# Two decoder blocks on one core: memory queries and second-block latents projected from unscaled chunks, and large tiles placed on multiples of 128 bytes

## The chip, the cores and the metric

One core of one Trainium2 chip runs the whole program. The metric is the device time of one execution in microseconds, lower is better. TensorE does the matrix products, VectorE (DVE) and ScalarE (ACT) the elementwise work, GpSimd (POOL) splits the weights, and SyncE (SP) issues the weight loads.

## What is computed

Two transformer blocks over 512 tokens of width 1024, all in float32. What matters here, cut down:

```python
h = x + token_mixers(rms_norm(x, norm_mix), ...)
n, mem_n = rms_norm(h, norm_mem), rms_norm(mem, norm_mem_kv)       # 512 and 256 tokens
h = h + memory_cross_attention(n, mem_n, w_mem_q, w_mem_kv, w_mem_o)
h = h + conv_ffn(rms_norm(h, norm_ffn), w_up, conv_w, conv_b, w_down)
x1 = rms_norm(h, final_norm)                                       # end of the first block
n2 = rmsnorm(x1, norm_g_2)                                         # start of the second
q_lat, c_kv, k_rope, z_a, ..., q_idx, k_idx, w_idx, ... = split(n2 @ w_in_2)
q  = rmsnorm(q_lat, g_q_lat_2) @ w_uq_2
kv = rmsnorm(c_kv, g_kv_lat_2) @ w_ukv_2
```

A norm multiplies each token by one number (its token scale, one over the root of the mean square) and each feature by a gain. The token scale commutes with the product by a weight matrix, so `norm(h) @ W` may be had as `((h * gain) @ W) * scale`.

## The kernel before

**Layout.** Activations lie feature-major: a tile holds 128 features on the partitions and 512 tokens along the row. A width of 1024 is 8 such chunks (`DC`), the width 2816 of the feed-forward part is 22 (`FC`).

**The products.** Every float32 operand of a projection is split into a high part (float32r) and the remainder, and `three` (L528 to L530) issues high x high, low x high and high x low for each pair of chunks, 128x128 weights against 512 tokens (256 in the memory's key and value projections). `project` (L536 on) makes one output chunk of 128 features from 8 input chunks, so 24 matmuls; `down` takes 22 input chunks, so 66 matmuls. Output chunks alternate between two PSUM banks. `open_bank` lets TensorE start chunk g only when chunk g-2 has been read by the engine that consumes it (`out_of_bank`).

**The weights.** They come as one stream of slots of 512 KB in exactly the order in which TensorE uses them, the table `STREAM`. SP loads into a ring of four, POOL makes `wH` (L483) and `wL` (L485) in two buffers each, preceded by a small `tick` (L482). POOL may split slot n+2 only when TensorE is through with slot n. All three orders (SP, POOL, TensorE) are the same table.

**The activations' split.** DVE writes a value to `nt` (two buffers), ACT copies it to the high tile (`high`, L1110), and DVE subtracts to make the low tile (`low`, L1524). TensorE waits for the low part of input chunk k before it uses it in a stage's first output chunk.

**A norm.** ACT squares the chunks (`squares`, L1078), DVE adds them up (`accumulate`, L1533), TensorE sums over the partitions with a matrix of ones (`norm_sum`, L513), ACT takes the root (`deviation`, L1085), DVE the reciprocal (`inverse`, L1542), and then DVE multiplies (`normed`, L1546, the helper `norm`).

**The order around the first part of the change.** `mix_out` (8 output chunks, inputs `mgH`, `mgL`) ends the token mixer. Beside it DVE first norms the memory tokens in eight chunks (with the residual of output chunk 0 ahead of memory chunk 4, L1896), then adds the residuals of chunks 1 to 7 (L1586 from L1897). TensorE goes on with stages `mem0` to `mem3`, one per head: two key chunks, two value chunks, a query chunk (j = 4), a transpose of values (j = 5), a query chunk (j = 6), a transpose (j = 7). The queries of head 0 need the normed hidden chunks `nH`, `nL`, which DVE makes after the sum over all eight residual chunks (L1898, L1899). ACT copies the query chunks out of PSUM to `mq` (L1348), in its queue ahead of the values' copy. Heads 1 to 3 are projected beside the attention of the head before (`mem_beside`). The feed-forward's norm is already done in the other way: `with_gain` (L1904) makes the chunks with the gain alone beside `mem_o`, and DVE applies the token scale to the products (L1923, L1930).

**The order around the second part.** `down` ends the first block. After each of its eight chunks DVE adds the residual (L1952), ACT squares it, DVE multiplies the chunk by the final gain in place (L1955), ACT squares it again, and DVE adds both squares to two sums (L1946). After the last chunk TensorE sums both over the partitions (L513, L956), DVE forms the variance for the two norms together (L1963, L1964), ACT takes the root (L1397), DVE the reciprocal (L1966), and then DVE and ACT make the eight split chunks `mix2` (L1969, L1110, L1524) for the first projection of the second block, `q_idx`. The order on TensorE is: two small products for the bias table (L962, L963), `q_idx` (2 output chunks), `w_idx`, `k_idx`, a transpose, `q_lat` (3), `c_kv` (2), `k_rope`, `z_a`. ACT copies the latents to `qlat` and `ckv`. DVE also rewrites `hT` as the first block's output (L1976).

**Where tiles lie.** `place` gives each SBUF tile the next address that is a multiple of 32 bytes. `hT`, `nH`, `nL`, the ring, `wH` and `wL` come first and lie at multiples of 128. Behind them comes `vec` of 680 bytes, so all others lie 64, 96 or 32 bytes past such a multiple: `mgH`, `moH`, `aH`, `recH`, `attH` and their low parts at 64, `yaH`, `ybH`, `mg2H`, `qlH`, `ckH` and theirs at 32.

Of the kernel before, what the change touches and what calls it, by code (L numbers as in the profile page):

```python
# [20 lines left out]
ALU = mybir.AluOpType  # L21
# [62 lines left out]
    ("q_idx", [1] * 2), ("w_idx", [1]), ("k_idx", [1]), ("w_turn", [0]), ("q_lat", [1] * 3), ("c_kv", [1] * 2),  # L84
# [145 lines left out]
def build(nc, stream, xT, memT, pos, vecs, ident_d, const_r, const_a, const_d, sink_d, relb_d, gvec, x1_d, outT):  # L230
    with ExitStack() as ctx:
# [25 lines left out]
        sq0 = -(-top[0] // 32) * 32  # L257
        sq = place("sq", [P, 2, S])
        sums0 = -(-top[0] // 32) * 32
# [3 lines left out]
        nt = place("nt", [P, 2, S])  # L263
        sgb = place("sgb", [P, 2, S])
# [6 lines left out]
        OVER = top[0]  # L271
# [61 lines left out]
        aL = place("aL", [P, FC, S], F32R)  # L333
        gpad = place("gpad", [P, 2, S + 2])
        cv = place("cv", [P, 2, S])
        fu = place("fu", [P, 2, S])
        sums2 = place("sums2", [P, S], at=229344 - 4 * S)
# [9 lines left out]
        rl0 = -(-top[0] // 32) * 32  # L347
        rl = place("rl", [P, 2, S])
        late0 = top[0]
# [52 lines left out]

        def c_a(name, a, b):
            return cA[:, AT_A[name] + a:AT_A[name] + b]
# [21 lines left out]
        hg_made, var_made = sem("hg_made"), sem("var_made")  # L426
# [20 lines left out]
        gv_done, gv_out = sem("gv_done"), sem("gv_out")  # L447

# [47 lines left out]
        def _(pe):  # L496
# [41 lines left out]
            def project(stage, c0, n, xs, width=S, inputs=None):  # L538


                for c in range(c0, c0 + n):
                    out = open_bank(FIRST[stage] + c)[:, :width]
                    for k, x in enumerate(xs):
                        if k % BLK == 0:
                            r = open_slot()
                        if inputs is not None and c == c0:
                            pe.wait_ge(nl_made, SPLIT[inputs] + k + 1)
# [420 lines left out]
            project("q_lat", 0, 3, n_parts)  # L968
            project("c_kv", 0, 2, n_parts)
# [75 lines left out]
        def _(act):  # L1045
# [288 lines left out]
            highs("memory", mnH, DC, MEM)  # L1334
            squares("mem", hT, residual("mix_out"))

            def mem_out(h, j):
# [8 lines left out]
                else:  # L1346
                    c = 2 * h + (j - 4) // 2
                    copy_out(stage, j, mq[:, c, :])  # L1348
# [3 lines left out]
            mem_out(0, 1)  # L1352
            for c in range(DC):
                high("mem", c, nH[:, c, :])
                if c in (2, 5):
                    mem_out(0, 2 + c // 3)
            for j in range(4, 8):
                mem_out(0, j)

            def mem_beside(x):  # L1360
                h = x // ST + 1
                if h < MEM_HEADS:
                    for j in ((0, 1), (2, 3), (4, 5), (6, 7))[x % ST]:
                        mem_out(h, j)
# [889 lines left out]
```

## Time and profile before

| what | value |
|---|---|
| median of 3 runs | 1625.26 us (1623.28 to 1625.79) |
| the profiled execution | 1619.58 us |
| its span, first to last instruction | 1617.8 us |
| TensorE busy | 1505.2 us, 93% of the span |
| VectorE busy | 1042.5 us, 64% |
| GpSimd busy | 856.2 us, 53% |
| ScalarE busy | 472.4 us, 29% |
| granted TensorE clock, mean | 0.982 of full speed |

The profile is of one execution. Its time is 1.8 us more than its span, and it lies 5.7 us under the median of the runs. Busy shares are averages over stages with different limits. A matmul's duration in the trace overlaps its successor's, so the time that one takes away from TensorE is the distance from one start to the next, and a TensorE that is called busy all the time may still issue faster or slower.

### The profile page before, as it was taken

What the parts mean: (1) busy time and instruction counts of PE and PEld (TensorE: products, weight loads), DVE (VectorE), ACT (ScalarE), POOL (GpSimd) and SP (SyncE); (2) the same over time, 40 slices, a digit from 0 to 9 for tenths busy, and PEclk for the clock granted to TensorE, in tenths of its full rate; (3) what the DMA queues carried; (4) which work ended last, traced back from release to release, by engine and by line L of the source; (5) the groups of instructions that cost most, each with busy time, mean ns of one, the idle gap of its engine ahead of it and who ended that gap; (6) DMA issues with size and microseconds to landing.
All of it is one profiled execution on the core that took longest, in us unless ns stands there. A gap on an engine that the chain in (4) does not pass through costs nothing.

```text
span 1617.8 us, 20168 instructions
## 1 busy us (share of the span) xinstructions
PE 1505.2 (93%) x6988; PEld 1170.7 (72%) x6988; DVE 1042.5 (64%) x1907; ACT 472.4 (29%) x908; POOL 856.2 (53%) x690
## 2 busy tenths in 40 slices
PE   5989999899999899999999999988989999999996
PEld 3878777566777688678888887865847677666874
DVE  7477797887256632489999982337187788576234
ACT  3455432356212222321011010012252334354111
POOL 3523322433665677266767677673637443433664
PEclk9999999999999999999999999998999999999998
DMA  5211111211332333133333333332413531322331
GB/s 203 79 52 40 40 40 40 65 53 53 105 91 86 90 109 106 53 92 91 92 95 101 93 102 98 103 103 92 129 52 91 104 92 53 117 66 73 123 91 65
DMA packets 38315, 138.48 MB, mean 86 GB/s; under 512 B 4312, under 2 KB 4568, under 8 KB 37592
## 3 DMA queue, kind: packets, MB, share of 16 engines
q1 hardware_dynamic: 33408, 121.65, 24.9%
q10 hardware_dynamic: 4824, 15.69, 3.6%
q8 instruction: 56, 0.92, 0.3%
q14 instruction: 27, 0.22, 0.0%
HBM read 130.51 MB, written 6.82 MB: 85 GB/s over the span
## 4 chain that ended last, share of the span: by engine, by line
PE 77%; DVE 14%; issue 3%; ACT 3%; POOL 1%; PEld 0%; PEldq 0%; DMA 0%; ACTq 0%; DVEq 0%; POOLq 0%
PE pair L528 21%; PE pair L530 20%; PE pair L529 20%; PE pair L768 3%; PE pair L796 3%; PE pair L780 2%; DVE nt L1546 2%; PE pair L622 2%; PE pair L623 1%; DVE rstd L1542 1%; DVE nL L1524 1%; PE pair L984 1%; DVE kk L1737 1%; PE pair L670 1%; POOL wL L485 1%
## 5 line engine op out<-in xcount | busy, mean ns | idle before, releaser
L485 POOL TENSOR_TENSOR wL<-ring,wH 128x1024 fp32r<-128x1024 f32 x228 | 565.9, 2482 | 19.0
L528 PE MATMUL pair<-nH,wH 128*128 128x512 f32 x1120 | 452.4, 404 | 33.3 <-DVE nL L1524 15.4
L530 PE MATMUL pair<-nH,wL 128*128 128x512 f32 x1120 | 440.0, 393 | 0.0
L529 PE MATMUL pair<-nL,wH 128*128 128x512 f32 x1120 | 440.0, 393 | 0.0
L482 POOL TENSOR_TENSOR tick<-tick 128x1 f32<-128x1 f32 x228 | 55.9, 245 | 725.2 <-PE pair L530 716.0
L528 PEld LDWEIGHTS pair<-nH,wH 128*128 128x128 f32 x1120 | 211.8, 189 | 107.9 <-issue 30.0
L530 PEld LDWEIGHTS pair<-nH,wL 128*128 128x128 f32 x1120 | 212.3, 190 | 45.6
L483 POOL TENSOR_SCALAR wH<-ring 128x1024 fp32r<-128x1024 f32 x228 | 243.2, 1067 | 0.0
L529 PEld LDWEIGHTS pair<-nL,wH 128*128 128x128 f32 x1120 | 212.7, 190 | 41.5 <-issue 1.0
L1376 ACT ACTIVATE sgb<-cv 128x512 f32<-128x512 f32 x22 | 14.0, 634 | 208.8 <-DVE cv L1927 208.8
L528 PE MATMUL pair<-aH,wH 128*128 128x512 f32 x176 | 69.7, 396 | 0.0
L530 PE MATMUL pair<-aH,wL 128*128 128x512 f32 x176 | 69.6, 395 | 0.0
L529 PE MATMUL pair<-aL,wH 128*128 128x512 f32 x176 | 69.5, 395 | 0.0
L1658 DVE TENSOR_TENSOR X<-E,qT 128x64 f32<-128x64 f32 x224 | 40.4, 220 | 39.8 <-ACT E L1158 39.6
L1524 DVE TENSOR_TENSOR aL<-nt,aH 128x512 fp32r<-128x512 f32 x22 | 61.1, 2780 | 0.0
L1952 DVE TENSOR_TENSOR hT<-pair,hT 128x512 f32<-128x512 f32 x8 | 5.5, 692 | 81.0 <-PE pair L530 81.0
L1533 DVE TENSOR_TENSOR sums<-sums,sq 128x512 f32<-128x512 f32 (+1 forms) x38 | 36.5, 961 | 32.3 <-ACT sq L1078 30.9
L1926 DVE SCALAR_TENSOR_TENSOR cv<-gpad,vec,cv 128x512 f32<-128x512 f32 x22 | 56.7, 2578 | 0.8
L1586 DVE TENSOR_TENSOR hT<-pair,hT 128x512 f32<-128x512 f32 x24 | 16.5, 690 | 58.7 <-PE pair L530 58.7
L1158 ACT ACTIVATE E<-pair 128x896 f32<-128x896 f32 (+1 forms) x40 | 35.4, 937 | 61.4 <-PE pair L623 61.4
L1231 ACT ACTIVATE dx<-dx,stat 128x128 f32<-128x128 f32 (+3 forms) x64 | 36.0, 563 | 59.2 <-DVE stat L1785 59.0
L622 PE MATMUL pair<-cR,lftH 128*128 128x128 f32 (+1 forms) x144 | 43.4, 329 | 10.0 <-ACT Sg L1168 5.8
(339 smaller groups left out, 2738.9 us busy)
## 6 DMA issues: line engine op xcount, KB each, us to landing
ring<-stream SPq DMA_DIRECT2D x228, 512.0 KB, 3.6
gvec<-gv ACTq DMA_DIRECT2D x1, 2560.0 KB
hT<-xT SPq DMA_DIRECT2D x4, 512.0 KB, 5.4
x_d<-hT ACTq DMA_DIRECT2D x1, 2048.0 KB, 7.8
toep<-gvec ACTq DMA_DIRECT2D x8, 256.0 KB, 3.4
hT<-x_d ACTq DMA_DIRECT2D x1, 2048.0 KB, 8.6
outT<-hT ACTq DMA_DIRECT2D x8, 256.0 KB, 2.2
landing<-const_r ACTq DMA_DIRECT2D x1, 1216.0 KB, 6.3
```

The costliest lines, as they stand in the source:

```text
L482: pool.tensor_tensor(tick[:, 1:2], tick[:, 0:1], tick[:, 0:1], ALU.add).then_inc(high_done, 1)
L483: pool.tensor_scalar(wH[:, r % SPL, :], ring[:, r, :], 1.0, 0.0, ALU.mult, ALU.add).then_inc(high_done, 1)
L485: pool.tensor_tensor(wL[:, r % SPL, :], ring[:, r, :], wH[:, r % SPL, :].bitcast(F32), ALU.subtract).then_inc(split_done, 1)
L528: mm(out, a[0], b[0], start=first, stop=False)
L529: mm(out, a[0], b[1], start=False, stop=False)
L530: return mm(out, a[1], b[0], start=False, stop=last)
L622: mm(out, lftH[:, d, i, :], m, start=first, stop=False)
L768: last = mm(out, *pairs[t], start=t == 0, stop=t == count - 1)
L796: last = mm(out[rows, qs], w, turned[:, j % 2, t, qs], start=n_t == 0, stop=n_t == len(kind["serves"]) - 1)
L1524: V.tensor_tensor(lo[:, c, :], nt[:, k % 2, :width], hi[:, c, :].bitcast(F32), ALU.subtract).then_inc(nl_made, 1)
L1658: last = V.tensor_tensor(two(X[:, m % 2, kind, xs])[:, half], E[:, n % 2, b, ls].rearrange("p (b c) -> p b c", c=c), two(src)[:, half], AL ...
L1926: own(V.scalar_tensor_tensor(out=y, in0=x[:, 0:S], scalar=w[0], in1=y, op0=ALU.mult, op1=ALU.add))
```

## The change

1. **Memory queries.** The chunks for the memory queries are made with the gain alone (`with_gain`, now for both norms), beside `mix_out`: chunks 0 and 1 after the memory's norm, the others each after its residual. ACT makes the high parts there. DVE takes the query products out of PSUM, multiplied by the token scale (`mem_query`), for head 0 after `inverse("mem")` and for the others beside the attention's steps 2 and 3. ACT's query copies are gone.
2. **Residuals.** The residuals of chunks 0 and 1 of `mix_out` come ahead of the memory's norm chunks 4 and 6. Before, only that of chunk 0 came there.
3. **Second block.** After each `down` chunk ACT writes `uH`, the chunk times both gains (`g12`), and DVE its low part `uL`. `q_lat` and `c_kv` are projected from these, in the order: `q_lat` 0, the sums over the partitions, `q_lat` 1 and 2, `c_kv` 0 and 1, then the bias table, `q_idx` and on as before. The two sums meet in one PSUM bank through a third product with a matrix that holds EPS, so that L1963 and L1964 go, and ACT takes the root from the bank. DVE takes the latents out of PSUM times the token scale: `q_lat` 0 before the chunks of `mix2`, `q_lat` 1 and 2 after chunks 1 and 4, `c_kv` after the last one. `hT` is multiplied by both gain and scale at the end in place of L1955 and L1976.
4. **Placement.** Tiles of 512 bytes and more start at multiples of 128 bytes.

```diff
-    ("q_idx", [1] * 2), ("w_idx", [1]), ("k_idx", [1]), ("w_turn", [0]), ("q_lat", [1] * 3), ("c_kv", [1] * 2),
+    ("q_lat", [1] * 3), ("c_kv", [1] * 2), ("q_idx", [1] * 2), ("w_idx", [1]), ("k_idx", [1]), ("w_turn", [0]),
...
+        def aligned(size=512):
+            step = 128 if size >= 512 else 32
+            return -(-top[0] // step) * step
...
-            off = -(-top[0] // 32) * 32 if at is None else at
+            off = aligned(size) if at is None else at
...
+            u_parts = [(uH[:, k, :], u_low(k)) for k in range(DC)]
+            project("q_lat", 0, 1, u_parts, inputs="unscaled")
             pe.wait_ge(sq_added, ADDED["mix2"] + CHUNKS["mix2"] - 1)
+            pe.wait_ge(eps_set, 1)
             norm_sum("final")
-            mm(bank(6), ones[:, :], sums2[:, :], start=True, stop=True).then_inc(sum_done, 1)
+            mm(bank(6), ones[:, :], sums2[:, :], start=True, stop=False)
+            mm(bank(6), eps[:, :], sums[:, :], start=False, stop=True).then_inc(sum_done, 1)
+            project("q_lat", 1, 2, u_parts)
+            project("c_kv", 0, 2, u_parts)
...
-            highs("memory", mnH, DC, MEM)
-            squares("mem", hT, residual("mix_out"))
+            for c in range(DC):
+                high("memory", c, mnH[:, c, :], MEM)
+                if c in (3, 5):
+                    squares("mem", hT, residual("mix_out"), chunks=[c // 2 - 1])
+            for c in range(DC):
+                if c >= 2:
+                    squares("mem", hT, residual("mix_out"), chunks=[c])
+                high("mem", c, nH[:, c, :])
...
+                A(uH[:, c, :], hT[:, c, :], ACT.Copy, scale=g12[:, c:c + 1]).then_inc(uh_made, 1)
...
-            norm("memory", memx, "norm_mem_kv", mnH, mnL, MEM, lambda c: residual("mix_out", "mem", [0]) if c == 4 else None)
-            residual("mix_out", "mem", range(1, DC))
+            norm("memory", memx, "norm_mem_kv", mnH, mnL, MEM,
+                 lambda c: residual("mix_out", "mem", [c // 2 - 2]) if c in (4, 6) else None)
+            scale_queries = with_gain("mix_out", "mem", "norm_mem")
+            for c in range(2):
+                scale_queries(c)
+            residual("mix_out", "mem", range(2, DC), scale_queries)
+            low("mem", DC - 1, nH, nL)
...
+            def mem_query(h, b):
+                bk, free = product(f"mem{h}", 4 + 2 * b)
+                V.tensor_tensor(mq[:, 2 * h + b, :], bk, rstd[:, :], ALU.mult).then_inc(free, 1)
...
-            norm("mem", hT, "norm_mem", nH, nL)
+            def mem_beside(x):
+                if x % ST >= 2 and x // ST + 1 < MEM_HEADS:
+                    mem_query(x // ST + 1, x % ST - 2)
...
-                V.tensor_scalar(hT[:, c, :], hT[:, c, :], vcol("final_norm", c), None, ALU.mult).then_inc(hg_made, 1)
+                V.scalar_tensor_tensor(out=u_low(c), in0=hT[:, c, :], scalar=g12[:, c:c + 1], in1=uH[:, c, :].bitcast(F32),
+                                       op0=ALU.mult, op1=ALU.subtract).then_inc(ul_made, 1)
...
+            scaled("q_lat", 0, qlat)
             for c in range(DC):
-                V.scalar_tensor_tensor(out=open_split("mix2", c), in0=hT[:, c, :], scalar=vcol("norm_g_2", c),
-                                       in1=sums[:, :], op0=ALU.mult, op1=ALU.mult).then_inc(nt_made, 1)
+                V.scalar_tensor_tensor(out=open_split("mix2", c), in0=hT[:, c, :], scalar=g12[:, c:c + 1],
+                                       in1=sums2[:, :], op0=ALU.mult, op1=ALU.mult).then_inc(nt_made, 1)
                 if c:
                     low("mix2", c - 1, nH, nL)
+                if c in (1, 4):
+                    scaled("q_lat", 1 + c // 4, qlat)
             low("mix2", DC - 1, nH, nL)
+            for c in range(2):
+                scaled("c_kv", c, ckv)
```

## Rows read from the trace of the kernel before

**Rows 1.** The page: the engines of the chain that ended last, shares of the span

```profile
PE 77%; DVE 14%; issue 3%; ACT 3%; POOL 1%; PEld 0%; PEldq 0%; DMA 0%; ACTq 0%; DVEq 0%; POOLq 0%
```

**Rows 2.** The view by stretches: busy time (instructions) of each engine, granted clock, DMA

```profile
core 0: us, PE busy (x) PEld busy (x) DVE busy (x) ACT busy (x) POOL busy (x), PEclk, DMA share, GB/s
...
530.00:570.00 40.00, 31.24 (x169) 24.34 (x168) 25.02 (x24) 10.94 (x21) 26.75 (x21) 0.91 0.31 92
...
735.00:962.00 227.00, 226.54 (x999) 187.23 (x998) 210.60 (x168) 23.77 (x41) 161.84 (x125) 1.00 0.32 95
...
1086.00:1115.00 29.00, 16.10 (x43) 8.64 (x43) 23.01 (x24) 8.21 (x14) 5.28 (x6) 0.71 0.23 78
```

**Rows 3.** The view by tile, TensorE: count, duration min/median/max ns, first and last start

```profile
L529 PE MATMUL pair<-nL,wH x328: 387/389/396, 739.8 to 962.2; 128*128 128x512 f32 x164
...
L529 PE MATMUL pair<-aL,wH x176: 393/394/400, 962.9 to 1085.5; 128*128 128x512 f32 x176
...
L529 PE MATMUL pair<-moL,wH x64: 394/394/396, 675.1 to 719.2; 128*128 128x512 f32 x64
...
L529 PE MATMUL pair<-mg2L,wH x64: 392/397/400, 1556.8 to 1601.8; 128*128 128x512 f32 x64
```

**Rows 4.** Waits of TensorE, 486 to 568 us: us in total, times, longest

```profile
PE pair L528 <- ACT vraw L1066: 4.3, 1, 4.3
PE pair L528 <- DVE hT L1586: 2.4, 2, 1.2
```

**Rows 5.** Timeline of head 0's first query chunk, its weights' split, and the first scores

```profile
543.37 2.69 POOL L485 TENSOR_TENSOR wL<-ring,wH 128x1024 fp32r<-128x1024 f32 x1
...
545.05 0.28 PE L530 MATMUL pair<-mnH,wL 128*128 128x256 f32 x1
549.64 0.79 PE L528 MATMUL pair<-nH,wH 128*128 128x512 f32 x1 [4.30 <-ACT vraw L1066]
...
555.27 0.60 PE L530 MATMUL pair<-nH,wL 128*128 128x512 f32 x1
...
567.66 1.10 PE L768 MATMUL pair<-mk,mq 128*128 128x256 f32 x4 [0.83 <-ACT mv L1066]
```

**Rows 6.** The view by line: scores of the memory attention, all heads

```profile
L768 PE MATMUL pair<-mk,mq 128*128 128x256 f32 x64 | 16.7, 384 | 2.7 <-ACT mv L1066 2.7
```

**Rows 7.** Timeline of VectorE at the end of `mem_o`, where chunks are made unscaled

```profile
719.84 0.69 DVE L1586 TENSOR_TENSOR hT<-pair,hT 128x512 f32<-128x512 f32 x1 [0.61 <-PE pair L530]
...
724.16 1.48 DVE L1533 TENSOR_TENSOR sums<-sums,sq 128x512 f32<-128x512 f32 x2
```

**Rows 8.** Timeline from the end of `down` to the end of `k_rope`

```profile
1086.20 0.69 DVE L1952 TENSOR_TENSOR hT<-pair,hT 128x512 f32<-128x512 f32 x1 [10.02 <-PE pair L530]
...
1087.59 2.34 POOL L485 TENSOR_TENSOR wL<-ring,wH 128x1024 fp32r<-128x1024 f32 x1
1087.75 2.46 DVE L1955 TENSOR_SCALAR hT<-hT,vec 128x512 f32<-128x512 f32 x1 [0.86 <-ACT sq L1393]
...
1091.66 2.08 PE L513 MATMUL pair<-sums,ones 128*128 128x512 f32 x2 [5.50 <-DVE sums L1946]
...
1095.33 0.69 DVE L1963 TENSOR_SCALAR sums<-pair 128x512 f32<-128x512 f32 x1 [3.72 <-PE pair L956]
...
1097.44 3.35 DVE L1966 RECIPROCAL sums<-std 128x512 f32<-128x512 f32 x1 [0.69 <-ACT std L1397]
...
1103.11 0.77 PE L528 MATMUL pair<-nH,wH 128*128 128x512 f32 x1 [5.02 <-DVE nL L1524]
...
1112.00 3.34 DVE L1542 RECIPROCAL rstd<-std 128x512 f32<-128x512 f32 x1
...
1163.10 0.60 ACT L1066 ACTIVATE kp<-pair 128x512 f32<-128x512 f32 x1 [4.84 <-PE pair L530]
```

**Rows 9.** Bounds: float32 products at full clock, and VectorE's low parts beside a busy GpSimd

```profile
631.58 3.60 PE L796 MATMUL pair<-mPT,mv 128*128 128x512 f32 x8
...
L1524 DVE TENSOR_TENSOR aL<-nt,aH 128x512 fp32r<-128x512 f32 x22 | 61.1, 2780 | 0.0
```

More of the change, by code:

```diff
@@ L270, in build @@
         warm = place("warm", [P, len(NORMS)])
-        OVER = top[0]
+        g12 = place("g12", [P, DC])
+        OVER = top[0] = aligned()
         cA = place("cA", [P, COLS_A])
@@ L1413, in _ @@
             act.wait_ge(gv_out, 2)
-            for c in range(3):
-                copy_out("q_lat", c, qlat[:, c, :])
             squares("q_lat", qlat, lambda c: out_of_bank(act, FIRST["q_lat"] + c))
-            for c in range(2):
-                copy_out("c_kv", c, ckv[:, c, :])
             copy_out("k_rope", 0, kp[:, :])
@@ L1913, in _, with with_gain, use @@
-            residual("mem_o", "ffn", after=with_gain)
+            def with_gain(stage, name, gain):
+                def use(c):
+                    out = open_split(name, c)
+                    out_of_bank(dve, FIRST[stage] + c)
+                    V.tensor_scalar(out, hT[:, c, :], vcol(gain, c), None, ALU.mult).then_inc(nt_made, 1)
+                    if c:
+                        low(name, c - 1, nH, nL)
+                return use
+            norm("memory", memx, "norm_mem_kv", mnH, mnL, MEM,
+                 lambda c: residual("mix_out", "mem", [c // 2 - 2]) if c in (4, 6) else None)
@@ L1914, in _ @@
+            for b in range(2):
+                mem_query(0, b)
+            def mem_beside(x):
+                if x % ST >= 2 and x // ST + 1 < MEM_HEADS:
+                    mem_query(x // ST + 1, x % ST - 2)
+            attention("memory", mx, MEM_SCALE, lambda i: nomask[:, :], moH, moL, beside=mem_beside)
+            residual("mem_o", "ffn", after=with_gain("mem_o", "ffn", "norm_ffn"))
             low("ffn", DC - 1, nH, nL)
+            V.tensor_tensor(g12[:, :], vec[:, VEC["final_norm"]:VEC["final_norm"] + DC],
+                            vec[:, VEC["norm_g_2"]:VEC["norm_g_2"] + DC], ALU.mult).then_inc(gains_made, 1)
@@ L1956, in _, with scaled @@
             add_squares(DC - 1)
-            dve.wait_ge(sum_done, NORMS.index("mix2") + 1)
-            own(V.tensor_scalar(sums[:, :], bank(7), EPS, None, ALU.mult))
-            V.tensor_tensor(sums2[:, :], bank(6), sums[:, :], ALU.add).then_inc(var_made, 1)
             dve.wait_ge(std_made, NORMS.index("final") + 1)
-            V.reciprocal(sums[:, :], std[:, :]).then_inc(r_made, 1)
+            V.reciprocal(sums2[:, :], std[:, :]).then_inc(r_made, 1)
             dve.wait_ge(r_made, NORMS.index("final") + 1)
+            def scaled(stage, c, dst):
+                b, free = product(stage, c)
+                V.tensor_tensor(dst[:, c, :], b, sums2[:, :], ALU.mult).then_inc(free, 1)
```

67 lines of the change are left out of this document (30 added, 37 removed).

## The prediction

> **What bounds the kernel now.** I read the chain that ended last first, since a busy share says nothing of what would shorten the run. TensorE holds 77% of it and DVE 14% [rows 1]: most of the time the matmuls set the pace, and in a few places DVE does. The view by stretches shows where. In `up` TensorE is busy for 226.54 of 227 us, although DVE works 210.60 us beside it; from 1086 to 1115 us it is busy for 16.10 of 29 us at a granted clock of 0.71, and from 530 to 570 us for 31.24 of 40 at 0.91 [rows 2]. These two low places are the ones that the change rearranges. Third, the tile view, for the price of a matmul that nobody delays. A count with first and last start gives the distance: in `up`, which reads `nL` and `nH`, (962.2 - 739.8) / 327 triples = 0.680 us, or 226.7 ns a matmul; in `down`, which reads `aL` and `aH`, (1085.5 - 962.9) / 175 = 0.7006, or 233.5 ns; in `mem_o` (719.2 - 675.1) / 63, or 233.3 ns [rows 3]. The weights' buffers are the same. What differs is where the moving tile lies: `nH` at a multiple of 128 bytes, the other two 64 past one, and `mg2L`, 32 past, has a duration of 397 ns against 389 [rows 3].
>
> **Part A, the memory stage.** (1) TensorE waits twice in `mix_out`, 1.2 us each, for the residual add that frees a bank [rows 4]: once for chunk 0's, once for chunk 1's, which stands behind all eight chunks of the memory's norm. The first stays where it was, the second now comes ahead of memory chunk 6, some 3 us sooner. Gain 1.2.
>
> (2) The value chunks end with the start at 545.05 plus 0.1, and head 0's first query chunk starts only at 549.64, a wait of 4.30 us for the normed chunks (the row names ACT's copy, but DVE is the one that is late); then it crawls, 15 matmuls from 549.64 to 555.27, 0.40 us from start to start, which is the lower of TensorE's two clock levels, 1.2 GHz [rows 5, 4]. The scores start at 567.66 [rows 5]. Afterwards the query chunks are all ready long before. What is late next is POOL's low weight: it ends at 543.37 + 2.69 = 546.06 [rows 5], so I start there. Two query chunks of 24 x 0.227 = 5.44 us, two transposes of some 0.4, a bank wait of 0.8 before the second (DVE's multiply, 0.7, and its hand-over) and 0.9 until queries and values are out give 546.1 + 10.9 + 0.8 + 0.8 + 0.9 = 559.5. Gain 8.2. The sum over the squares, at which TensorE stops between the first two key chunks, ends later: DVE has a gain and a low part more per chunk. In `mem_o`, which is this same order, the last square is added 724.16 + 1.48 - 719.84 = 5.8 us after the last residual [rows 7]; here that is 536.2, and TensorE arrives at 537.5. So it costs nothing, with 1.3 us to spare; if a blocked add used that up, 1 us would be lost. The work beside `mix_out` (a gain, a low part and an add per 5.6 us chunk) is hidden too, as `mem_o` shows: its 192 matmuls run at 233.3 ns without a hole [rows 3].
>
> (3) With the query copies off ACT's queue, the values' copy starts sooner. All the scores wait 2.7 us for it in sum [rows 6]; 0.8 of that is head 0's, counted above. A copy of 0.6 goes, but half of it ran beside the transpose. I take 1.0 for the three other heads, bounds 0 and 1.9. The new waits stand on DVE: `mem_query` waits for TensorE with the next `normalise` behind it, but the transposes of these probabilities come three steps later, and the next row maximum follows the same TensorE chunk. Cost 0; if ACT's exponents slipped and its bank copies with them, 0.5 for each of 12 steps.
>
> A: 1.2 + 8.2 + 1.0 = 10.4 us, bounds 6 and 12.
>
> **Part B, the second block's start.** Before, `down` ends at 1086.2 (the residual's start), and the copy of `k_rope` starts at 1163.10, so its products end at 1162.9 [rows 8]: 76.7 us. In it are ten projections, 10 x 5.44 = 54.4 us. The other 22 are the chain squares, sums (1091.66), variance (1095.33, two operations), root, reciprocal (1097.44), first chunks, first matmul at 1103.11 [rows 8], and then a crawl at DVE's pace: eight chunk pairs between the reciprocal's end at 1100.8 and the next one at 1112.00, 1.40 us each [rows 8], partly at the lower clock [rows 2].
>
> Afterwards: `q_lat` 0 starts at 1086.2, its weights are split. `uL` of the last chunk needs the residual (0.69), ACT's copy (0.63) and DVE's subtraction, which starts at about 1087.65, just behind POOL's `wL` at 1087.59. L1955 at 1087.75 took 2.46 us where POOL's took 2.34 [rows 8], so I let it end at 1090.5. TensorE wants it after 21 matmuls, at 1091.0: hidden, with 0.5 to spare. `q_lat` 0 ends at 1091.65. The two last adds end at 1091.9, and TensorE goes on at 1092.0 with three float32 products of two passes; eight passes take 3.60 us with the last one's tail [rows 9], 0.43 each, so 2.6 us, of which 0.9 is new: 1094.6. Root and reciprocal, 0.1 + 0.6 + 0.1 + 3.35 [rows 8], end at 1099.0. `q_lat` 0 is out at 1099.7, and `q_lat` 2, which needs its bank, can start when `q_lat` 1 ends, at 1100.05. From there TensorE has four projections until 1116.5 and 1.3 us for the bias table, which its loads have long reached: 1117.8.
>
> DVE in that time: eight pairs at 1.40 = 11.2 [rows 8], two latents at 0.7 = 1.4, one `c_kv` 0.7, so 13.3, and 1113.0 without a rival. But POOL was idle here before (5.28 of 29 us busy [rows 2]) and now is not: a `wL` of 2.4 us falls after each projection, and DVE's operations on two SBUF tiles wait for it. Three fall on the way at some 2.2 each: 1119.6. `q_idx` cannot open its bank before `c_kv` 0 is read, and that stands behind all of `mix2` on DVE, so `q_idx` 0 starts at 1119.6 and TensorE idles 1.8 us. What follows has its inputs: five projections and a transpose, 27.2 + 0.8, end `k_rope` at 1147.6. Gain 1162.9 - 1147.6 = 15.3. One blocked operation more makes it 13, none 17.
>
> Moved work that costs nothing: the slots' order in SP and POOL moves with TensorE's, with no slot more; ACT's `uH` copy (0.63) and DVE's `uL` lie in the 15 us that a `down` chunk leaves them; the rewrite of `hT` comes after `mix2` and ends near 1135, while ACT asks for it behind `k_idx`, near 1141; the norms of the latents hang on `z_a`, so their waits shift with it unchanged.
>
> **Part C, the placement.** All moving tiles of 512 columns come to multiples of 128. By the code these are the reads of `aH`, `aL` 528, `mo` 192, `mg` 192, `mg2` 192, `rec`, `att`, `ya`, `yb` 96 each, `ql` 54 and `ck` 48: 1590 matmuls. At 233.4 - 226.7 = 6.7 ns [rows 3] this is 10.7 us. In all these stages TensorE sets the pace but for some edges, so I take 10. DVE, ACT and POOL tiles move as well; no row separates their durations by place, so 0, bounds -1 and 3.
>
> Here a rule speaks against this part. The Trainium skill, SBUF — State Buffer, section Door 1: The DMA port swizzle, states cachelines of 16 bytes. A start 64 or 32 bytes past a multiple of 128 already opens a line, so by that rule C would give 0. The rows differ by 6.7 ns at both offsets, so I go by them, and keep the rule as a rival.
>
> **The sum.** 10.4 + 15.3 + 10 = 35.7 us. The profiled execution took 1619.6 us, so 1583.9; it lies 5.7 us under the median of the runs, 1625.3, and by that median the forecast is 1589.6 us. I say 1589.5.
>
> **The rivals.** (i) The placement gives nothing: the 6.7 ns come from something else that differs between `up` and `down`. For it: only `nH`, `nL` lie well, so place and tile are not separated. Against it: DVE is far busier in `up`, and six other tiles at two offsets share the slower pace. Gain 25.7, time 1599.6. By the rule of the Trainium skill's page SBUF — State Buffer above this is the outcome. (ii) DVE becomes the bound at the block's start. In `up`, with POOL busy, a low part takes 2780 ns on average [rows 9]; were all eight of `mix2` so, the chain would be 8 x (0.75 + 2.78) + 2.1 = 30.3 us from 1099.0, so 1129.3, and B would be 15.3 - 9.7 = 5.6: time 1599.2. Against it: in `up` a POOL split is nearly always on when a low part comes, since DVE falls into step with it. Halfway, 1594. (iii) The queries are no earlier, because a query chunk meets POOL's pace or the sum over the partitions is late: A is 4 instead of 10.4, time 1596. (iv) Slower than before: with every large tile at the same place within 128 bytes, the engines' reads meet in SBUF, and projections pay for it. Today `nt`, `sq` and `sums` lie 64 bytes off `nH`. A and B give 25.7, so the 4950 matmuls of 512 columns would have to take 5.2 ns more than `up`'s 226.7 each for no gain, and from 5.9 on the kernel is over 0.2% slower. At 8 ns, 1639. Against it: 389 ns has a spread of 387 to 396 beside a DVE that is 93% busy [rows 3, 2]; nothing shows such meetings. (v) The moves don't do what they say: a bank order puts the old waits back. The order of banks was followed above and gives only the `c_kv` wait.
>
> **How the numbers follow.** Forecast 0.70; (i) 0.09; (ii) in part or whole 0.11; (iii) 0.06; (iv) 0.02; (v) 0.02. The forecast's own bounds, A 6 to 12, B 13 to 17, C 9 to 14, give 1582 to 1597; the rivals (i) to (iii) reach 1600. Range 1582 to 1601. A measurement can tell 0.2%, or 3.2 us, from no change. Faster 0.97, same 0.01, slower 0.02.
>
> **What would show it.** Right: the tile view has 389 ns for `aL`, `moL` and `mg2L`, and `down` lasts 119.7 instead of 123.3 us; the clock from `down` to `k_rope` is 1.00; `q_idx` starts within 4 us of the end of `c_kv`; the wait for `vraw` of 4.3 us is gone and one of the two waits for `hT`; the scores start about 14.5 us after the end of the value chunks. Wrong: aligned tiles still at 394 ns (C), a wait of over 5 us of `q_idx` for `ckv` (B), a new wait of `norm_sum` for `sums` in either place, or a distance over 230 ns in `up` (the rival on the slower side).

## The result, and the profile of the changed kernel

The changed kernel takes 1600.98 us (median of 4 runs, 1599.46 to 1608.38), the kernel before 1624.27 us beside it: ratio 0.9861, interval 0.9838 to 0.9885. The forecast was 1589.5 us, 35.7 us less than before; 23.3 us were measured. Sign and places were right, the size was not: the measured time lies at the far end of the forecast's range, and near the 1599.6 us of its first rival, that the placement gives nothing, which came true only in part. The profiled execution took 1602.36 us, 17.2 us less than that of before.

The page and its chain: TensorE holds 76% (77% before [rows 1]), DVE still 14%.

```profile
span 1600.6 us, 20168 instructions
...
PE 76%; DVE 14%; issue 4%; ACT 3%; POOL 2%; PEld 0%; PEldq 0%; DMA 0%; ACTq 0%; DVEq 0%; POOLq 0%
```

The view by stretches, for the places of [rows 2], each moved with its stage, and one shorter stretch:

```profile
523.00:563.00 40.00, 35.35 (x196) 29.59 (x195) 22.84 (x17) 6.85 (x15) 30.45 (x25) 1.00 0.37 111
729.00:956.00 227.00, 226.54 (x999) 187.25 (x999) 210.68 (x167) 23.74 (x41) 162.50 (x125) 1.00 0.32 95
1080.00:1109.00 29.00, 27.98 (x115) 21.21 (x114) 24.09 (x19) 8.35 (x13) 19.33 (x15) 1.00 0.40 132
1112.00:1120.00 8.00, 6.14 (x20) 4.14 (x20) 7.87 (x8) 0.63 (x1) 4.42 (x3) 0.79 0.32 107
```

Both low places filled up: TensorE is busy for 35.35 of 40 us where it was for 31.24, and for 27.98 of 29 us where it was for 16.10, at a granted clock of 1.00 instead of 0.91 and 0.71. The last row is what is left of the second one, at 0.79.

TensorE by tile (`nL` in `up` only), which answers to [rows 3]:

```profile
L544 PE MATMUL pair<-nL,wH x329: 389/389/395, 732.9 to 956.7; 128*128 128x512 f32 x165
...
L544 PE MATMUL pair<-aL,wH x176: 387/393/404, 957.4 to 1079.6; 128*128 128x512 f32 x176
...
L544 PE MATMUL pair<-moL,wH x64: 390/393/404, 669.7 to 713.7; 128*128 128x512 f32 x64
...
L544 PE MATMUL pair<-mg2L,wH x64: 389/389/393, 1540.8 to 1584.6; 128*128 128x512 f32 x64
```

`mg2L` has the 389 ns that part C promised, `aL` and `moL` have not: (1079.6 - 957.4) / 525 = 232.8 ns a matmul in `down`, where it was 233.5 before and 226.7 was expected, though the tiles lie at multiples of 128 bytes. The prediction had named aligned tiles at 394 ns as the sign against part C.

The waits of TensorE from `mix_out` to the first scores (480 to 562 us, [rows 4]):

```profile
PE pair L543 <- POOL wL L500: 2.9, 3, 1.1
PE pair L543 <- DVE mgL L1539: 1.9, 2, 1.2
PE pair L543 <- DVE hT L1601: 0.9, 1, 0.9
```

The 4.3 us for `vraw` are gone. A residual is still waited for, and the timelines of POOL, DVE and TensorE show which (each row is of one of them):

```profile
505.69 2.45 POOL L500 TENSOR_TENSOR wL<-ring,wH 128x1024 fp32r<-128x1024 f32 x1
...
505.81 3.01 DVE L1916 TENSOR_SCALAR nt<-hT,vec 128x512 f32<-128x512 f32 x2
...
509.73 0.68 DVE L1601 TENSOR_TENSOR hT<-pair,hT 128x512 f32<-128x512 f32 x1
...
510.47 0.51 PE L543 MATMUL pair<-mgH,wH 128*128 128x512 f32 x1 [0.92 <-DVE hT L1601]
```

It is chunk 2's, for which chunk 4 waits: DVE makes the unscaled chunks 0 and 1 first (L1916), and is held up behind POOL's `wL` in doing so.

The timeline of the second block's start, against [rows 8] (PE, DVE, POOL, ACT by time; a row with x2 holds two instructions). L498 makes `wH` and L500 `wL` of a weights' slot, L2006 a chunk of `mix2`, L1539 its low part, and L2002 takes a latent out of its bank:

```profile
1080.31 0.69 DVE L1986 TENSOR_TENSOR hT<-pair,hT 128x512 f32<-128x512 f32 x1 [9.70 <-PE pair L545]
...
1086.12 1.12 PE L528 MATMUL pair<-sums,ones 128*128 128x512 f32 x2 [0.30 <-DVE sums L1980]
...
1088.39 0.80 PE L543 MATMUL pair<-uH,wH 128*128 128x512 f32 x1
...
1089.63 3.35 DVE L1997 RECIPROCAL sums<-std 128x512 f32<-128x512 f32 x1 [3.56 <-ACT std L1416]
...
1095.05 1.05 POOL L498 TENSOR_SCALAR wH<-ring 128x1024 fp32r<-128x1024 f32 x1
...
1095.07 1.57 DVE L1539 TENSOR_TENSOR nL<-nt,nH 128x512 fp32r<-128x512 f32 x1
...
1096.18 2.72 POOL L500 TENSOR_TENSOR wL<-ring,wH 128x1024 fp32r<-128x1024 f32 x1
...
1097.16 2.29 DVE L2006 SCALAR_TENSOR_TENSOR nt<-hT,g,sums 128x512 f32<-128x512 f32 x1
...
1100.86 1.50 POOL L498 TENSOR_SCALAR wH<-ring 128x1024 fp32r<-128x1024 f32 x1
...
1101.48 1.41 DVE L2006 SCALAR_TENSOR_TENSOR nt<-hT,g,sums 128x512 f32<-128x512 f32 x1
...
1102.44 2.72 POOL L500 TENSOR_TENSOR wL<-ring,wH 128x1024 fp32r<-128x1024 f32 x1
...
1102.81 2.89 DVE L1539 TENSOR_TENSOR nL<-nt,nH 128x512 fp32r<-128x512 f32 x1
...
1106.23 1.30 DVE L2006 SCALAR_TENSOR_TENSOR nt<-hT,g,sums 128x512 f32<-128x512 f32 x1
...
1107.08 2.71 POOL L500 TENSOR_TENSOR wL<-ring,wH 128x1024 fp32r<-128x1024 f32 x1
...
1107.45 2.88 DVE L1539 TENSOR_TENSOR nL<-nt,nH 128x512 fp32r<-128x512 f32 x1
...
1114.48 1.28 DVE L2002 TENSOR_TENSOR ckv<-pair,sums 128x512 f32<-128x512 f32 x2
1115.68 3.33 DVE L1557 RECIPROCAL rstd<-std 128x512 f32<-128x512 f32 x1
...
1115.21 0.80 PE L543 MATMUL pair<-nH,wH 128*128 128x512 f32 x1 [1.85 <-DVE ckv L2002]
...
1145.27 0.60 ACT L1087 ACTIVATE kp<-pair 128x512 f32<-128x512 f32 x1 [3.05 <-PE pair L545]
```

From the last residual to `k_rope`'s copy it is 64.96 us instead of 76.90: part B is worth 11.9 us, not 15.3. `q_idx` waits 1.85 us for the bank of `c_kv` 0.

**Where the difference lies.** Distances in us: before, changed, and the same changed kernel in a second profiled execution, r1. A stage goes from its first matmul to the first one of the next, but for these: the recurrence is taken from the first product with `X` to the first with `qa`, the attention of block 1 from there to the first scores and from the first product with `recH` to the first with `attH`; `down` ends with the start of the last residual; `out2` and the attention of block 2 (the scores of `kb` and `qb`) end with the start of their own last matmul. Other stages are left out.

```
                                      before  changed      r1
recurrence                            148.20   148.26  154.23
attention of block 1, first part       76.74    77.56   77.00
attention of block 1, second part     104.76   105.51  105.25
mix_out                                49.25    50.23   48.81
memory keys, values, queries           37.51    29.74   29.78
memory attention                      106.77   106.49  106.40
mem_o and up                          288.25   288.05  288.05
down                                  123.52   123.15  123.17
last residual to k_rope                76.90    64.96   65.05
attention of block 2                   85.31    88.51   87.46
b's mixing products                    55.14    54.40   54.40
out2                                   45.47    44.19   44.25
```

The change alters no instruction of the recurrence and of the two attentions, only places of tiles, and their lengths differ between two executions of one kernel as well. That concerns the comparison of single profiles and comes back below.

### The profile page after: what moved, and what is told of

The parts are those of the page before. It is cut to its first block, busy times and chain, and to the rows that moved or that the text cites. A ratio compares the mean times of both kernels' runs of the same rounds, so it can differ in the third digit from the quotient of the medians.

```text
span 1600.6 us, 20168 instructions
## 1 busy us (share of the span) xinstructions
PE 1502.6 (94%) x6990; PEld 1174.4 (73%) x6990; DVE 1055.9 (66%) x1920; ACT 470.6 (29%) x903; POOL 859.1 (54%) x690
## 4 chain that ended last, share of the span: by engine, by line
PE 76%; DVE 14%; issue 4%; ACT 3%; POOL 2%; PEld 0%; PEldq 0%; DMA 0%; ACTq 0%; DVEq 0%; POOLq 0%
PE pair L543 21%; PE pair L545 20%; PE pair L544 20%; PE pair L785 3%; PE pair L813 3%; PE pair L797 2%; PE pair L639 2%; PE pair L640 1%; DVE nL L1539 1%; DVE rstd L1557 1%; PE pair L1005 1%; DVE nt L1561 1%; DVE dx L1794 1%; POOL wL L500 1%; DVE kk L1752 1%
## 5 line engine op out<-in xcount | busy, mean ns | idle before, releaser
L500 POOL TENSOR_TENSOR wL<-ring,wH 128x1024 fp32r<-128x1024 f32 x228 | 566.2, 2483 | 19.0
L543 PE MATMUL pair<-nH,wH 128*128 128x512 f32 x1080 | 434.5, 402 | 25.3 <-DVE nL L1539 8.6
L545 PE MATMUL pair<-nH,wL 128*128 128x512 f32 x1080 | 423.7, 392 | 0.0
L544 PE MATMUL pair<-nL,wH 128*128 128x512 f32 x1080 | 423.4, 392 | 0.0
L543 PEld LDWEIGHTS pair<-nH,wH 128*128 128x128 f32 x1080 | 204.1, 189 | 92.7 <-issue 25.4
L498 POOL TENSOR_SCALAR wH<-ring 128x1024 fp32r<-128x1024 f32 x228 | 244.9, 1074 | 0.0
L545 PEld LDWEIGHTS pair<-nH,wL 128*128 128x128 f32 x1080 | 204.3, 189 | 44.0
L544 PEld LDWEIGHTS pair<-nL,wH 128*128 128x128 f32 x1080 | 204.5, 189 | 40.8 <-issue 1.0
L1539 DVE TENSOR_TENSOR aL<-nt,aH 128x512 fp32r<-128x512 f32 x22 | 61.1, 2781 | 0.0
L1986 DVE TENSOR_TENSOR hT<-pair,hT 128x512 f32<-128x512 f32 x8 | 5.5, 692 | 78.6 <-PE pair L545 78.6
L1539 DVE TENSOR_TENSOR nL<-nt,nH 128x512 fp32r<-128x512 f32 x32 | 56.4, 1763 | 0.6 <-ACT nH L1131 0.3
L1812 DVE TENSOR_SCALAR dx<-dx,stat 128x128 f32<-128x128 f32 (+3 forms) x64 | 48.6, 759 | 2.3
```

Source lines behind the costliest of these rows:

```text
L498: pool.tensor_scalar(wH[:, r % SPL, :], ring[:, r, :], 1.0, 0.0, ALU.mult, ALU.add).then_inc(high_done, 1)
L500: pool.tensor_tensor(wL[:, r % SPL, :], ring[:, r, :], wH[:, r % SPL, :].bitcast(F32), ALU.subtract).then_inc(split_done, 1)
L543: mm(out, a[0], b[0], start=first, stop=False)
L544: mm(out, a[0], b[1], start=False, stop=False)
L545: return mm(out, a[1], b[0], start=False, stop=last)
L1539: V.tensor_tensor(lo[:, c, :], nt[:, k % 2, :width], hi[:, c, :].bitcast(F32), ALU.subtract).then_inc(nl_made, 1)
```

## The experiments

Each is an edit of the changed kernel, but for r3. "Distance" is the time from one matmul's start to the next, as in the prediction. All ratios are to the kernel before, run beside it.

**r1: the changed kernel again.** No edit.

> The changed kernel itself, as the common yardstick of this call. Both theories: 1599 to 1604 us, 0.985 to 0.988 of before. Its large tiles of the first block lie at 0 modulo 512, those of the second block at 384, nH, nL and the weights at 128.

1601.99 us (1599.13 to 1608.1), ratio 0.9858 (0.9824 to 0.9893): the 23 us stand. Its own kernel before has a median of 1628.15 us, so that here the medians lie 26.2 us apart; the gain of the whole is known to some 4 to 6 us either way. In its profile `mix_out` is 1.4 us shorter than in the first one, where six matmuls in a row are 0.43 us apart, and the recurrence is 6.0 us longer.

**r2: the first block's tiles 128 bytes further.**

```diff
-        OVER = top[0] = aligned()
+        OVER = top[0] = aligned() + 128
```

> The changed kernel with all tiles of the first block 128 bytes further (128 modulo 512 in place of 0), those of the second block unmoved. Theory P (the price of a moving tile hangs on its place modulo 256: 128 is fast, 0 is slow): aL, mgL, moL, uH go from a start distance of 232 ns to 227 ns, median duration from 393 to 389; 1104 matmuls of the first block and 120 of uH at 5.3 ns are 6.5 us, so 1593 to 1597 us. Rival B (the second block's tiles are fast for another reason than place, such as a quieter VectorE): no change, 232 ns, 1601 us.

TensorE by tile in r2:

```profile
L544 PE MATMUL pair<-aL,wH x176: 388/390/398, 962.3 to 1082.3; 128*128 128x512 f32 x176
...
L544 PE MATMUL pair<-moL,wH x64: 387/389/391, 675.7 to 718.6; 128*128 128x512 f32 x64
```

A distance of 42.9 / 189 = 227.0 ns in `mem_o`, and `down` is 120.86 us long instead of 123.15. So the first block can have `up`'s pace, and a multiple of 128 is not what gives it. The whole kernel took 1601.16 us (0.9845, 0.9814 to 0.9876), so the pace came as expected and the 1593 to 1597 us did not: the gain is smaller than what its runs differ by (1595.76 to 1604.88), but the fastest is 3.4 us below r1's, which is what the stages add up to (2.3 and 1.1).

**r3: the placement alone, on the kernel before**, at the changed kernel's addresses.

```diff
+        def aligned(size=512):
+            step = 128 if size >= 512 else 32
+            return -(-top[0] // step) * step
...
-            off = -(-top[0] // 32) * 32 if at is None else at
+            off = aligned(size) if at is None else at
```

> The kernel before with the placement alone, at the very addresses that the changed kernel has. Theory P: the second block's 486 matmuls with moving tiles at 384 modulo 512 gain 6.7 ns each, 3.3 us, the first block's 1104 gain 1 ns, 1 us: 4 us less than before, 1619 to 1622. Theory of the prediction (multiples of 128 all fast): 10 us less. Rival B: the same as before within 1 us.

1625.34 us, ratio 0.9986 (0.9963 to 1.001): by itself the placement can't be told from nothing in the whole time (2.8 us by the medians), where the forecast gave it 10 us. Its stages do show it: `down` takes 123.15 us, `b`'s mixing products 54.40 and `out2` 44.19, the changed kernel's values.

**r4: the change without the placement.**

```diff
-            step = 128 if size >= 512 else 32
+            step = 32
-        OVER = top[0] = aligned()
+        OVER = top[0]
```

> The changed kernel with tiles at multiples of 32 bytes as before (the first block's at 96 modulo 128, the second's at 64). Parts 1 to 3 stay. By the trace of the changed kernel they carry 19 us, so 1603 to 1607 us; all of these moving tiles at 233 to 234 ns, nL at 227. If the parts add up to more with the placement than without (VectorE's durations hang on it too), 1608 or more.

1604.7 us (0.9874, 0.9842 to 0.9906), 2.7 above r1, as expected. `b`'s mixing products take 55.10 us again and `out2` 45.31, so in these stages the 0.7 and 1.1 are the placement's.

**r5: the first block 256 bytes further**, as r2 with `+ 256`.

> The changed kernel with the first block's tiles 256 bytes further: 256 modulo 512. Theory P with period 256: aL, mgL, moL, uH stay at 232 ns from start to start, as at 0. Theory P with period 512: 227 ns. The second block's tiles (384) stay at 227 in both.

The distance in `down` is 232 ns, as with 0 bytes, and the kernel took 1607.63 us in its single run. Thus 128 and 256 bytes differ, and 0 and 256 don't.

**r6: everything behind `nH` and `nL` moved**: 128 bytes ahead of `ring` move weights and both blocks' tiles, while `nH` and `nL` stay.

```diff
+        top[0] += 128
         ring = place("ring", [P, RAW, BLK * P])
```

> The changed kernel with 128 bytes between nL and the ring, so that the ring, wH, wL and all behind them lie 128 further: weights at 256 modulo 512, the first block's moving tiles at 128, the second block's at 0, nH and nL unmoved at 128. Theory P-absolute (the moving tile's own place modulo 256 decides): nL 227, aL 227, mg2L 232 ns. Theory P-relative (the distance to the weights' tile modulo 256 decides): nL 232, aL 232, mg2L at 256 from the weights 227 ns. Under the second the whole kernel would be some 3080 x 5 = 15 us slower than the changed one.

TensorE by tile in r6 (`nL` in `up` only):

```profile
L545 PE MATMUL pair<-nL,wH x325: 390/393/404, 748.2 to 974.1; 128*128 128x512 f32 x163
...
L545 PE MATMUL pair<-aL,wH x176: 390/393/404, 974.8 to 1097.0; 128*128 128x512 f32 x176
...
L545 PE MATMUL pair<-mg2L,wH x64: 389/389/402, 1559.8 to 1603.6; 128*128 128x512 f32 x64
```

This decides it. `nL` was not moved, and it lost its pace: 393 ns, 225.9 / 972 = 232.4 ns from start to start. `mem_o` and `up` together take 293.63 us instead of 288.05, the kernel 1621.42 in a single run. Over all six placements one number orders these stages, the distance in bytes between the moving tile and the weights' tile:

```
distance modulo 256      stages                                  ns a matmul
0                        up in all but r6; down, mem_o in r2;
                         out2 in after, r2, r6                   227
128                      down, mem_o in after, r3, r5, r6;
                         up in r6                                232
32, 64 or 96 past a
multiple of 128          down, mem_o, out2 in before, r4         233 to 234
```

Two limits. `att_mix`, with `attH` at distance 128 in the changed kernel, takes 233.3 ns there as it did before, and reaches 226.7 in r2. And the ring always lay at the same place modulo 256 as `wH` and `wL`, so that the runs don't say which of the three counts. `nt` and the sums are out of it: in the kernel before, `aH` lay at their place modulo 256 and was slow, and `nH` did not and was fast.

**r7: the memory part as before** (parts 1 and 2 undone).

```diff
-            norm("memory", memx, "norm_mem_kv", mnH, mnL, MEM,
-                 lambda c: residual("mix_out", "mem", [c // 2 - 2]) if c in (4, 6) else None)
-            scale_queries = with_gain("mix_out", "mem", "norm_mem")
...
+            norm("memory", memx, "norm_mem_kv", mnH, mnL, MEM, lambda c: residual("mix_out", "mem", [0]) if c == 4 else None)
+            residual("mix_out", "mem", range(1, DC))
+            inverse("mem")
+            norm("mem", hT, "norm_mem", nH, nL)
```

> The changed kernel with parts 1 and 2 undone (memory queries and residuals as before), the second block's start and the placement kept. My account: from the first mgH matmul to the first scores 86.8 us as before in place of 80.0; from there to the first moH matmul 0.3 longer. Total 1607 to 1612 us. Rival: the memory part is worth nothing because GpSimd's weights set the pace there, under 2 us of difference.

The waits of TensorE in r7, 486 to 568 us:

```profile
PE pair L543 <- ACT vraw L1087: 4.3, 1, 4.3
PE pair L543 <- DVE hT L1603: 2.5, 2, 2.3
```

The old wait is back, and the stage of keys, values and queries has 37.48 us again: part A(2) is 7.7 us there. The whole does not say so: 1603.2 us (0.9855, 0.9819 to 0.9892), under the 1607 to 1612 that were expected, 1.2 above r1 by the medians and 3.7 by the fastest of each. By the medians alone its rival, under 2 us, is what was seen; what speaks against it is the stage. In its profile `mix_out` takes 53.27 us, 4.0 more than in the kernel before with the same order (the wait of 2.3 us, and matmuls 0.43 us apart behind it and behind an earlier wait), and the attention of block 2 is the shortest of all (84.97, before 85.31, all others from 87.4 up). So how much of the 7.7 us the end keeps is open; no wait that a trace names takes them back later.

**r8: three edits together**, one for each wait or pace that the readings above had left: r2's placement, `c_kv` 0 taken from its bank behind chunk 6 of `mix2`, and residual 2 ahead of the unscaled chunks.

```diff
-            for c in range(2):
-                scale_queries(c)
-            residual("mix_out", "mem", range(2, DC), scale_queries)
+            residual("mix_out", "mem", [2])
+            for c in range(3):
+                scale_queries(c)
+            residual("mix_out", "mem", range(3, DC), scale_queries)
...
+                if c == 6:
+                    scaled("c_kv", 0, ckv)
             low("mix2", DC - 1, nH, nL)
-            for c in range(2):
-                scaled("c_kv", c, ckv)
+            scaled("c_kv", 1, ckv)
```

> The changed kernel with the first block's tiles at 128 modulo 512, c_kv 0 taken out of its bank after chunk 6 of mix2 instead of after chunk 7's low part, and the residual of mix_out chunk 2 ahead of the two unscaled chunks. If the c_kv bank is what q_idx waits for, its wait of 1.9 us goes and q_idx starts within 0.5 us of the bias table's products; if VectorE's whole chain of mix2 is the bound, TensorE waits for nL instead, by as much. In mix_out the wait of 0.9 for hT goes, or turns up at the next chunk. From the first mgH to the first mnH matmul 49.2 us (1.0 less; with the placement's 1.0), from the end of down to the start of q_idx 33.2 in place of 35.1. Total 3 us under the run with the placement alone moved, 1593 to 1599 us, less than the executions of one kernel differ by.

1590.38 us (1590.04 to 1597.35), ratio 0.9785 (0.9755 to 0.9815), the fastest of all, and under the 1593 to 1599 that were expected. The wait for `ckv` is not in its list of waits any more, `down` has 120.86 us. Its waits in `mix_out` (482 to 531 us), with r1's below (487 to 537):

```profile
PE pair L543 <- DVE hT L1601: 1.6, 2, 1.4
```

```profile
PE pair L543 <- DVE hT L1601: 1.9, 2, 1.2
```

So `mix_out` still waits for residuals. In r8 these are 1.4 us for chunk 0's and 0.2 for chunk 3's, in r1 1.2 for chunk 0's and 0.7 for chunk 2's. The stage takes 48.29 us instead of 48.81, and its 192 matmuls at the faster pace would be worth 1.0 by themselves, so no gain is shown for the residual's move. The stages from `mix_out` to `k_rope` give 7.4 us against r1, the fastest runs lie 9.1 apart, the medians 11.6; the rest is open.

**r9: the second block as before** (part 3 undone, memory part and placement kept): the order of `q_lat`, `c_kv` and the index projections, L1963 and L1964, and the multiplication of `hT` behind each `down` chunk are back.

```diff
-            project("q_lat", 0, 1, u_parts, inputs="unscaled")
-            project("q_lat", 1, 2, u_parts)
-            project("c_kv", 0, 2, u_parts)
...
+            project("q_lat", 0, 3, n_parts)
+            project("c_kv", 0, 2, n_parts)
```

> The changed kernel with its second-block part undone: the latent projections stand behind the index projections again, the norm's variance is finished by VectorE, nothing is taken unscaled there; the memory part and the placement stay as changed. The theory (the part is worth the 11.9 us that the profiled pair shows between the last down chunk's addition, rows 8, and the copy of k_rope): that distance goes back to 76 to 78 us, the stage from aH to down's end stays within 0.5 us of 123.0, and the kernel takes 1611 to 1615 us, 11 to 13 above the changed one. The rival (what B gains is taken back later, at the attention over k_idx, so that it shows less in the total): the distance goes back all the same, but the total lies only 5 to 9 us above the changed kernel, at 1605 to 1609, and the stretch from k_rope to the block's attention is shorter by the difference.

The two ends of the part in r9:

```profile
1084.11 0.69 DVE L1973 TENSOR_TENSOR hT<-pair,hT 128x512 f32<-128x512 f32 x1 [10.01 <-PE pair L537]
...
1160.90 0.60 ACT L1073 ACTIVATE kp<-pair 128x512 f32<-128x512 f32 x1 [4.84 <-PE pair L537]
```

76.8 us, against 64.96: 11.8. The kernel took 1612.28 us (0.9905, 0.9876 to 0.9934), 11.3 above the changed one, 10.3 above r1, and 8.5 by the fastest of each. The times alone would leave room for the rival, that part of B is taken back later (5 to 9 us). The stages don't: from `k_rope`'s copy to the first scores of the second block's attention it is 92.03 us here, 92.04 and 91.34 in the two profiles of the changed kernel, so nothing is given back there.

**r10: `c_kv` 0 earlier, alone**, the second edit of r8.

> The changed kernel with one edit: VectorE takes c_kv 0 from its bank behind chunk 6 of mix2's norm, not behind chunk 7 with c_kv 1. The theory (TensorE waits for that bank for about 1.9 us, and q_idx and k_idx start later by it): the stage from cD, relb to k_idx's end is shorter by 3 to 3.5 us than 51.7, as it was with all three edits together, so all of that belongs to this one, and the kernel takes 1596 to 1598 us. The rival (the chunks of mix2 that VectorE hands over later by one operation take the wait's place; the gain came from the first block's tiles, 128 bytes further): the stage is within 1 us of 51.7 and the kernel within 1 us of 1601.

1596.13 us (1595.53 to 1605.09), ratio 0.9814 (0.9772 to 0.9857). From the bias table's first product to the first product over the index keys (L1005), 51.58 to 51.84 us in six profiles that keep the old place and 51.07 in r6, it is 48.43 here and 48.30 in r8. So the bank wait costs 3.3 us, though it lasts 1.9: with it goes the slow start behind it, six matmuls 0.43 to 0.60 us apart from 1115.21 on, in the row 1112 to 1120 above with its clock of 0.79.

## Why the prediction was right and wrong

The steps against the stages (us; "changed" by r1 where the first profile has a stretch at the lower clock that r1 has not):

```
step                            predicted  measured  from
A(1) residual waits                   1.2       0.4  mix_out 49.25, 48.81
A(2) queries ready earlier            8.2       7.8  37.51, 29.74; r7 37.48
A(3) query copies off ACT             1.0       0.3  memory attention
B    second block's start            15.3      11.9  76.90, 64.96; r9 76.8
C    placement                       10         2.9  down 0.4, mem_o 0.2, then
                                                     0.4 in uq and ukv, 0.7 in
                                                     b's mixing, 1.2 in out2
sum                                  35.7      23.3  medians: 23.3
```

The sum agrees with the medians, which is partly luck, for those of r1 lie 26.2 apart. What failed first was the size of two terms, C and B; A(1) and A(3) are small, and each came to a third of its price.

**C failed by its rule.** "All moving tiles of 512 columns come to multiples of 128" was true and did not matter. [Rows 3] held one fast tile and three slow ones and could not tell "at a multiple of 128" from "at the same place as the weights", which lay at a multiple of 128 as well. The price, 6.7 ns, was right where the distance became 0 modulo 256: the second block's 486 matmuls would be 3.3 us by it and gave 2.3. The first block's 1104 matmuls, with distance 128, gave 0.6 us instead of 7.4. The rival of 0.09, placement gives nothing, came nearest for that block, and for the wrong reason. The Trainium skill, SBUF — State Buffer, section Door 1: The DMA port swizzle, states lines of 16 bytes. 128 and 256 bytes are both whole numbers of these, so by that alone the two would be alike; r2 and r5 differ by 5 ns a matmul, and the runs decide.

**B was right up to the reciprocal, and then short by 3.4.** `q_lat` 1 was to start 8.4 us after the last residual and starts 8.1 after it (1088.39), the reciprocal 9.3 where 9.2 was forecast. From the reciprocal's end `c_kv` 0 was to be read within 20.6 us and is within 22.1, so that `q_idx` starts 34.9 us after the residual instead of 33.4. The three operations blocked behind `wL` are there, 1.6, 2.2 and 2.2 us longer than the 0.7 of a free one (rows 1097.16, 1102.81, 1107.45), together the 6.6 of the forecast less 0.6. Not in it was POOL's other operation on the weights, `wH` (L498), which holds DVE up as well: by 0.9 at 1095.07, and twice more by some 0.6 each (1101.48, 1106.23). These 2.1 less the 0.6 are the 1.5. The other 1.9 I had not priced at all: TensorE, idle for 1.85 us, starts at the lower clock, and `q_idx` to `k_rope` takes 29.9 us where 28.0 was forecast. Without the wait, in r10, it takes 1.4 less, so 1.4 of the 1.9 is the slow start; the other 0.5 was not traced to a row. (A slip without effect: the forecast's own terms put the reciprocal's end at 1098.75, not at 1099.0.) The wait itself was forecast, as 1.8 us; what it does to the matmuls behind it was not, though [rows 5] showed a crawl behind just such a wait. The blocking agrees with what the Trainium skill's page SBUF — State Buffer, section SBUF: two separate sides, says of VectorE and GpSimd: an operation of one holds the shared ports until it ends. The blocked rows start inside a POOL operation and end 0.5 to 0.6 us behind it.

**A(1) left out the work ahead of residual 2.** Residual 1 does come earlier, and its wait of 1.2 us is gone; chunk 0's stays, 1.2 in r1. But the new work of step (2), the unscaled chunks 0 and 1, stands ahead of residual 2, and one of its operations is blocked behind POOL: 3.01 us for two at 505.81, and residual 2 is what TensorE waits for next, 0.9 us (0.7 in r1). I had taken the work beside `mix_out` as hidden, "as `mem_o` shows"; `mem_o` does each chunk behind its own residual, with no backlog of two. That residual 2 ahead of them would win this back is not shown (r8).

**A(2) holds:** the scores start 29.7 us after the stage's start, 7.8 us of the 8.2 predicted. What is late now is `wL`, as the prediction had it: its three waits, 0.9, 1.0 and 1.1 us, stand ahead of key and value chunks.

**A(3) put its new wait at nothing.** "The new waits stand on DVE", with cost 0. The scores' wait for ACT's values copy, 2.7 us in four [rows 6], is gone, and in its place they wait for DVE's query multiply (555 to 660 us):

```profile
PE pair L785 <- DVE mq L1932: 1.7, 4, 0.6
```

That leaves 0.3 us of the 1.0.

**The rivals.** (ii), DVE becomes the bound at the block's start, happened in a small part: DVE's chain ends 1.5 us later than forecast, far from the 9.7. (iii), queries no earlier, is refuted by the stage and by r7. (iv) is refuted by `up`, whose distance stayed at 227 ns at the changed placement. (v) didn't happen but for A(1)'s new order; besides the `c_kv` wait, `c_kv` 1 waits 0.7 us for `q_lat` 2's bank, ahead of the point where DVE is the later one anyway.

**Profile against profile.** The two first profiles differ by 17.2 us and the medians by 23.3. The 6.1 between are stages that the change leaves alone or that r1 has shorter: 0.8 and 0.7 in the attention of block 1, 1.4 in `mix_out`, 3.2 in the attention of block 2. The prediction knew that its profiled execution was 5.7 us under the median and put that on as one sum; the stages show where such a difference sits.

## What to carry to other kernels

Before a tile is moved for its address, write down the addresses of both operands of the matmul, and look for a pair of rows that differ in one of them only; a rule drawn from the moving tile alone would have been refuted by one run with the first block 128 bytes further. Where an early read gets rid of a wait, ask which operation now stands between the wait's end and the next bank: taking `c_kv` 0 out one norm chunk sooner was worth 3.3 us, a line's move. And price a wait of TensorE with the slower matmuls behind it, not by its length.

## What the hardware showed that was not expected

**Operand addresses.** Matmuls of 512 float32 columns go at 227, 232 or 233 to 234 ns each by the distance of the two operands' tiles in SBUF (0; 128; or 32, 64 and 96 past a multiple of 128, all modulo 256), 2 to 3% of a stage in which TensorE never waits; `att_mix` at 128 is the exception, with 233.3. Why this is so was not tried; other distances were not either.

**The clock in the recurrence.** The same instructions take 148.2 or 153 to 157 us, by the execution. The view by stretches, the recurrence in before's profile, and in r2's with two stretches of it:

```profile
86.72:234.92 148.20, 135.28 (x754) 115.22 (x753) 112.50 (x374) 69.89 (x89) 44.14 (x34) 0.98 0.15 43
```

```profile
86.74:243.53 156.79, 143.91 (x753) 122.92 (x752) 109.31 (x376) 69.89 (x89) 41.73 (x34) 0.92 0.14 41
...
125.00:135.00 10.00, 9.83 (x49) 9.22 (x50) 6.46 (x9) 1.94 (x2) 0.00 (x0) 0.66 0.01 2
180.00:190.00 10.00, 10.00 (x50) 9.12 (x50) 6.78 (x10) 1.94 (x2) 0.00 (x0) 0.66 0.00 0
```

The same work (754 and 753 matmuls) takes 8.6 us more at a mean granted clock of 0.92 instead of 0.98. In both short stretches of r2 TensorE is busy nearly all the time at a clock of 0.66; before has 1.00 there. Of twelve profiled executions, four have the short stage (148.2 to 148.4 us) and eight a longer one (153.3 to 157.1). What starts these stretches is open: TensorE's waits in the stage are the same within 0.1 us in both profiles (5.8 us for `Sg`, 3.0 for `lev`, 2.0 for `E`, 2.0 for `lftL`). Runs of one kernel spread by 9 to 12 us, nearly as much as part B is worth, and stretches like these can account for most of it, though only the profiled execution of each kernel shows them. A stage of a kernel is therefore best compared with the same stage.
